# A two-layer encoder with routed experts on one core: whole expert weights in one load, separate bias rows, last rows' loads from ACT, and a first group by columns

## The chip, the cores and the metric

One Trainium2 chip, one of its cores. The time is the device time of one execution in microseconds (us). Lower is better.

## The reference

Two layers over 256 tokens of width 1024, all in float32. Each layer normalises the rows, multiplies them by w_in (1024 x 2304), lets three groups of heads attend (A: a neighbourhood on a grid 64 wide with a learned bias; B: dilated windows; C: grouped queries with rotary positions), and adds the mixed heads times w_out. Then a router picks one of four groups of experts per token and two of the eight experts in it. Every expert is a gated pair of products:

```python
def expert_block(args):
    e, idx = args
    xb = xt[idx]
    return (jax.nn.silu(xb @ w_gate[e]) * (xb @ w_up[e])) @ w_down[e]
...
for l in range(DEPTH):
    x = x + mixer_sublayer(x, norm1_g[l], w_in[l], ..., na_rpb[l], mix_norm_g[l], w_out[l])
    x = x + hier_moe(rms_norm(x, norm2_g[l]), ..., w_gate[l], w_up[l], w_down[l])
```

w_gate and w_up are 1024 x 512 per expert, w_down is 512 x 1024; each is 2 MB, there are 32 experts in a layer, and all of them are loaded. That is 403 MB of expert weights in two layers; everything else is some 33 MB.

## The kernel before, in words

**Memory.** SBUF holds a ring of 16 pieces of 1 MB (8 KB in each of 128 partitions) and, beside it, six regions of the same size that are free once the attention part is over: three in `work`, then `tables`, `biased` and `hT`. `rows` (line 324) gives the memory of a piece; pieces 16 to 21 are those six.

**Items.** The experts of a layer are worked through in 11 items. `KINDS` and `TIME` (lines 75 and 79) give the number of experts in the order of work: 2, 2, 4, 1, 4, 1, 4, 2, 4, 4, 4. Each item has up to 128 places for tokens, shared by its experts. An item has six rounds, the upper and the lower half of w_gate, w_up and w_down, and needs one piece per round and expert. TensorE (PE) gathers the tokens by a matmul with a one-hot matrix (line 951), runs the six rounds (line 989), and brings the result back to x (line 1015). ACT takes the Silu of the gate rounds and copies, VectorE (DVE) makes the one-hot matrices (lines 1715 to 1719), multiplies, and adds to x (line 1750). The six rounds of four experts are 32 matmul instructions each.

**The plan.** `ring_plan` (line 102) is run when the program is built. It deals out the pieces in the order of loading: each load gets the piece that is free first, with the semaphore and value that say so (`p_round` counts rounds, `p_down` the last round's halves, five and two per item). Items up to the eighth may use pieces 0 to 20, later ones 0 to 15. SP issues every load from this plan, in order (`item`, line 529; `piece_in`, line 447, lines 449 to 453 being the waits and the load); a load that has to wait for its piece holds back all that follow. PE waits for the landings of all experts' pieces at the start of a round (line 983). A few pieces around the second and third item are loaded in halves (`half_in`, line 455).

**The last item.** Here PE also runs matmuls with the identity between the rounds (`warm`, line 671). The lower half of w_down comes in three parts (`lower_half_in`, line 467, issued at line 476): the two chunks of rows with the first 512 columns, then one chunk with the other 512, then the other chunk. PE takes the first part at once (`lower_rows`, line 997, matmuls at line 1007), brings back the first half of the result, and then takes the other two.

**The attention part.** w_in is loaded in three groups of 768 columns, C, A and B, 3 MB each, into three adjoining pieces. A group comes as two loads of half the rows (line 515), but the very first one, of layer 1, as four: by columns (the key and value columns 512 to 768, then the query columns 0 to 512) and by halves of the rows (lines 502 to 511). A projection runs in units; the first two use the key and value columns, the next two the query columns (`project`, line 694). The learned bias of group A is built from windows of the rows of na_rpb, each partition reading 250 numbers per head, one number further on than the partition before (`bias_loads`, line 417), which PE spreads by a matmul with a flip matrix (line 727). For layer 1 that is 64 x 4 rows of 250 numbers; for layer 2 it is 64 rows of 1645 numbers, from the first head's window through the last one's, loaded during the last but one item of layer 1 (`staged_loads`, line 408). The router's decisions come from PE, DVE and ACT; before the ranks of the tokens (line 943) PE runs three `warm` calls.

**Order of work.** The engines' programs are written out by hand, the same for both layers, with the semaphores named in the code: `mixers`, `first`, ten items, a loop for experts with too many tokens (not entered with these inputs), and the eleventh item. SP's order of loads in a layer is: w_in's groups with the small tables between them, w_out, then the expert weights.

Of the kernel before, what the change touches and what calls it, by code (L numbers as in the profile page):

```python
# [29 lines left out]
P = 128  # L30
# [8 lines left out]
GRID = 64  # L39
# [52 lines left out]
BESIDE_FREE = [("p_pv", 8, 24)] * 4 + [("p_logit", 2, 40), ("p_pv", 8, 24)]  # L92
TABLES, BIASES, TURNED_ROWS, EARLY = PIECES + 2, PIECES + 3, PIECES + 4, PIECES + 5
# [5 lines left out]
HALVED = {(l, *key): 2 * l + n for l in range(LAYERS) for key, n in (((1, 5, 0), 1), ((1, 5, 1), 2), ((2, 0, 0), 2))}  # L99


def ring_plan():
# [6 lines left out]
    def take(key, n, done, time, allowed):  # L109
        starts = [i for i in allowed if i + n <= max(allowed) + 1 or n == 1]  # L110
# [12 lines left out]
    for l in range(LAYERS):  # L123
# [29 lines left out]
def encoder(nc, a, out):  # L153
    ctx = ExitStack()
    with ctx:
# [12 lines left out]
        tables = sb("tables", [P, PIECE])  # L168
        biased = sb("biased", [P, PIECE])
# [75 lines left out]
        head_step = [250, 465]  # L245
# [3 lines left out]
        beside = [work[:, 0:PIECE], work[:, PIECE:2 * PIECE], tables[:], biased[:], hT_flat, work[:, 2 * PIECE:3 * PIECE]]  # L249
# [106 lines left out]

        block = ctx.enter_context(nc.Block())
# [32 lines left out]
        def _(sp):  # L390
# [26 lines left out]
            def bias_loads(l):  # L417

                first = a["na_rpb"][l:l + 1, 0:1, 4:11, 0:GRID // 2 - 1]
                lo = 15 - (GRID - 1)  # L420
                shape = [[GRID, 4, 250], [GRID, 1, 3 * 465 + 250]][l]
                sp.dma_start(windows[l].rearrange("p (h c) -> p h c", h=shape[1]),
                             bass.AP(first.tensor, first.offset + lo, [[1, GRID], [465, shape[1]], [1, shape[2]]])).then_inc(d_rel, 16)
# [54 lines left out]
            def mixers(l):  # L478
# [4 lines left out]
                for g in range(3):  # L483
# [18 lines left out]
                    if l == g == 0:  # L502

                        for n, (c0, c1) in enumerate(PARTS["C"]):
                            src = a["w_in"][l:l + 1, :, lo + c0:lo + c1].rearrange("l (k p) c -> (l p) k c", k=KD)
                            for half in range(2):
                                ks = slice(half * 4, half * 4 + 4)
                                sp.dma_start(group_in(l, g)[:, ks, c0:c1], src[:, ks]).then_inc(d_lower[n] if half else landed[pos + n], 16)
                                if n == half == 0:
                                    sp.dma_start(x[:, 1], xr[:, 1]).then_inc(d_x[1], 16)  # L510
# [11 lines left out]
                if l:  # L522
                    dil_load(l)
                    route_loads(l)

# [3 lines left out]
            def item(l, i, q):  # L529
# [9 lines left out]
                for r in range(6):  # L539
                    for e in range(n):  # L540
# [7 lines left out]
                        if (l, i, r, e) in HALVED:  # L548
# [4 lines left out]
                            if (i, e) != (1, 1):  # L553
                                half_in(l, i, r, e, ids[e], 1)
                        elif r < 5 or i < NI - 1:
# [1286 lines left out]
```

## Time and profile before

| | us |
|---|---|
| median of 3 runs | 1176.21 |
| lowest and highest | 1175.89, 1178.5 |
| the profiled execution | 1178.81 |
| its span, first to last instruction | 1177.0 |
| TensorE (PE) busy | 997.6 |
| VectorE (DVE) busy | 327.1 |
| ScalarE (ACT) busy | 170.9 |
| GpSimd (POOL) busy | 51.6 |
| bytes moved | 436.80 MB, 371 GB/s on the mean |

The chain of work that ended last has 57% of the span on PE, 31% on loads and 7% on SP's queue. In the rows further down, L12 is line 12 of the kernel, "PEclk" the granted clock of TensorE as a share of full speed, "DMA share" the mean busy share of the 16 DMA engines, and `SPq` the instructions of SP's sequencer, the issues of loads above all; an issue that lasts long is one that was held back. "x32" counts instructions, and a float32 matmul is two of them. The time in square brackets is the engine's idle time before the row and what ended it.

### The profile page before, as it was taken

The numbers are of one execution on the slowest core, as the hardware profiler recorded it, in microseconds if no ns is written. First come the engines' busy times: TensorE is split into PE (matmuls) and PEld (weight loads), VectorE is DVE, ScalarE is ACT, GpSimd is POOL, SyncE is SP. The second block draws the span as 40 slices with busy tenths as digits, with TensorE's granted clock in tenths as the row PEclk, the third lists the DMA queues.
The fourth block names the chain that finished last, engine by engine and source line by source line (L and its number), as shares of the span: only waits on it lengthen the run. The fifth ranks groups of instructions, "written<-read, shape, count | busy, mean of one in ns | idle before, by whom it ended". The sixth has DMA issues, their size and how long they took to land.

```text
span 1177.0 us, 14082 instructions
## 1 busy us (share of the span) xinstructions
PE 997.6 (85%) x5406; PEld 467.7 (40%) x5406; DVE 327.1 (28%) x742; ACT 170.9 (15%) x440; POOL 51.6 (4%) x104
## 2 busy tenths in 40 slices
PE   8999999998977946659899999999969779474686
PEld 5556644353423412114356656444424234131242
DVE  3546543221211200102145555432212112010111
ACT  1344311110000100000014333111100001000000
POOL 2121100000000000000021211000000000000000
PEclk9999999999998987878999999999999989788899
DMA  9863889999999999999998247999999999999997
GB/s 307 331 250 114 351 305 416 421 421 420 422 422 420 420 422 356 420 422 421 406 399 305 104 178 286 357 417 420 421 421 422 420 421 421 422 420 422 421 421 281
DMA packets 78132, 436.80 MB, mean 371 GB/s; under 512 B 12800, under 2 KB 15792, under 8 KB 30704
## 3 DMA queue, kind: packets, MB, share of 16 engines
q1 hardware_dynamic: 78064, 435.87, 91.6%
q8 instruction: 45, 0.74, 0.2%
q14 instruction: 23, 0.19, 0.0%
HBM read 434.79 MB, written 1.05 MB: 370 GB/s over the span
## 4 chain that ended last, share of the span: by engine, by line
PE 57%; DMA 31%; SPq 7%; DVE 2%; issue 1%; POOL 1%; DVEq 0%; ACT 0%; POOLq 0%
PE bank L989 27%; DMA ring<-in_w_up 12%; DMA ring<-in_w_down 11%; PE bank L713 9%; PE bank L951 5%; SPq L453 5%; PE bank L840 5%; PE bank L1015 4%; DMA ring<-in_w_gate 2%; DMA biased<-in_w_down 2%; DMA tables<-in_w_down 2%; DMA ring<-in_w_in 1%; SPq L476 1%; PE bank L786 1%; PE bank L776 1%
## 5 line engine op out<-in xcount | busy, mean ns | idle before, releaser
L989 PE MATMUL bank<-ring,work 128*32 128x512 f32 (+2 forms) x2592 | 483.4, 671 | 153.3 <-DMA ring<-in_w_up 59.8
L989 PEld LDWEIGHTS bank<-ring,work 128*32 128x32 f32 (+2 forms) x2592 | 145.3, 131 | 427.9 <-issue 425.9
L713 PE MATMUL bank<-ring,hT 128*128 128x512 f32 (+1 forms) x384 | 128.3, 488 | 2.4 <-DMA ring<-in_w_in 1.2
L951 PE MATMUL bank<-work,h 128*128 128x128 f32 x704 | 89.9, 284 | 6.6 <-DVE work L1716 5.1
L951 PEld LDWEIGHTS bank<-work,h 128*128 128x128 f32 x704 | 85.2, 198 | 21.9 <-issue 15.2
L713 PEld LDWEIGHTS bank<-ring,hT 128*128 128x128 f32 x384 | 71.3, 190 | 49.9 <-issue 42.2
L1746 DVE COPY work<-bank 128x512 f32<-128x512 f32 x22 | 15.2, 691 | 253.6 <-PE bank L989 251.2
L1015 PE MATMUL bank<-work 128*128 128x512 f32 x176 | 81.4, 604 | 2.4 <-ACT work L1294 1.6
L1736 DVE TENSOR_TENSOR work<-work,bank 128x512 f32<-128x512 f32 x22 | 15.1, 687 | 238.4 <-PE bank L989 238.4
L1750 DVE TENSOR_TENSOR x<-x,bank 128x512 f32<-128x512 f32 x88 | 60.5, 687 | 44.3 <-PE bank L1015 44.3
L840 PE MATMUL bank<-ring,h 128*128 128x512 f32 x128 | 58.2, 600 | 0.0
L989 PE MATMUL bank<-work 128*32 128x512 f32 (+2 forms) x176 | 57.5, 594 | 0.0
L1289 ACT COPY work<-bank 128x512 f32<-128x512 f32 x22 | 12.9, 585 | 273.9 <-PE bank L1057 273.9
L1015 PEld LDWEIGHTS bank<-work 128*128 128x128 f32 x176 | 31.8, 190 | 50.9 <-issue 49.2
L1283 ACT COPY work<-bank 128x256 f32<-128x256 f32 x22 | 8.2, 372 | 299.3 <-PE bank L1039 299.3
L1715 DVE TENSOR_TENSOR work<-iota,work 128x512 f32<-128x512 f32 x20 | 13.8, 692 | 126.4 <-PE bank L1039 125.1
L989 PE MATMUL bank<-biased,work 128*32 128x512 f32 (+1 forms) x80 | 40.6, 655 | 0.0
L1294 ACT COPY work<-bank 128x512 f32<-128x512 f32 x22 | 12.9, 585 | 177.2 <-PE bank L989 159.9
L674 PE MATMUL bank<-ident 128*128 128x384 f32 x94 | 36.2, 531 | 2.8 <-DMA ident<-in_c_ident 2.8
L989 PE MATMUL bank<-hT,work 128*32 128x512 f32 (+1 forms) x80 | 36.3, 597 | 0.0
L989 PE MATMUL bank<-tables,work 128*32 128x512 f32 (+2 forms) x80 | 36.1, 594 | 0.0
L1272 ACT ACTIVATE work<-bank,gain 128x128 f32<-128x128 f32 x88 | 25.1, 368 | 57.9 <-PE bank L951 57.9
(206 smaller groups left out, 708.8 us busy)
## 6 DMA issues: line engine op xcount, KB each, us to landing
ring<-in_w_gate SPq DMA_DIRECT2D x110, 1024.0 KB, 26.0
ring<-in_w_up SPq DMA_DIRECT2D x108, 1024.0 KB, 26.7
ring<-in_w_down SPq DMA_DIRECT2D x100, 1024.0 KB, 26.5
ring<-in_w_in SPq DMA_DIRECT2D x10, 1536.0 KB, 14.8
work<-in_w_up SPq DMA_DIRECT2D x10, 1024.0 KB, 10.3
ring<-in_w_out SPq DMA_DIRECT2D x8, 1024.0 KB, 16.9
work<-in_w_gate SPq DMA_DIRECT2D x8, 1024.0 KB, 17.2
ring<-in_w_down SPq DMA_DIRECT2D x16, 512.0 KB, 12.1
```

What stands on the lines that cost most here:

```text
L453: sp.dma_start(rows(pos, k), w[:, 0, half * k:half * k + k]).then_inc(landed[pos], 16)
L674: matmul(bank[b][:, 0:3 * P].rearrange("p (n s) -> p n s", n=3), ident[:], ident[:].unsqueeze(1).broadcast_to([P, 3, P]), start=True, stop ...
L713: last = matmul(bank[6 + i % 2][:, 0:c1 - c0], hT[:, k, t * P:t * P + P], group_in(l, gi)[:, k, c0:c1], start=(k == 0), stop=(k == KD - 1))
L840: last = matmul(bank[6 + n % 2][:, :], mixed[:, pos0 + c, t * P:t * P + P], rows(pos, 2)[:, c % 2, half * 512:half * 512 + 512], start=(c ...
L951: last = nc.tensor.matmul(bank[k // 4][:, k % 4 * P:k % 4 * P + P], h_kc[:, t, k, :], pick[:, t, :], start=(t == 0), stop=(t == TT - 1))
L989: last = nc.tensor.matmul(bank[b][e * w:e * w + w, :], lhs[:, k, e * w:e * w + w], rows(pos, k_count // 2)[:, kk, n * 512:n * 512 + 512], ...
L1015: last = nc.tensor.matmul(bank[2 + n][:, :], pickT[:, t, :], y[:, half * 512:half * 512 + 512], start=True, stop=True)
L1272: last = nc.scalar.mul(xg[:, k, :], bank[1][:, (k - 4) * P:(k - 3) * P], gain2[:, q // NI, k:k + 1])
L1715: seated(tt(hot, over(iota[:, 0:P], 1, 2 * TT), wide(seats[:, TIME[i], :], P), ALU.is_equal))
L1736: tt(hid, hid, bank[3][:, :], ALU.mult).then_inc(v_hid, 1)
L1746: nc.vector.tensor_copy(y[:, 512:1024], bank[7][:, :]).then_inc(v_y, 1)
L1750: tt(xs, xs, bank[2 + n][:, :], ALU.add).then_inc(v_back[n], 1)
```

## The change

- From the fourth item on, the two halves of a weight are loaded by one instruction of 2 MB (`whole_in`), into two adjoining pieces, and both are free again only after the second half's round. In the last item that holds for w_gate alone. Where all of an item's six loads were one piece each, pieces 0 to 15 can be paired, and 16 with 17 and 18 with 19; piece 20 takes no whole weight. `tables` and `biased` become one tensor `kept`, so that they adjoin. PE waits for a whole weight at its first round and for nothing at its second.
- SP copies layer 2's bias windows, 64 x 4 rows of 250 numbers, to a region `apart` in device memory during layer 1, after w_out's loads; the load for layer 2 reads 64 rows of 1000 numbers from there, after a wait for the copy.
- The third part of the last item's lower w_down half is issued by ACT and no longer by SP, after the Silu and the third round, with ACT's own reads of the experts' numbers.
- The first group of w_in is loaded by columns in layer 2 too.
- PE runs four `warm` calls, not three, before the ranks, and two short matmuls with the identity after them.

```diff
+WHOLE_FROM = 3
+def whole(i, r):
+    return i >= WHOLE_FROM and (i < NI - 1 or r < 2)
...
     def take(key, n, done, time, allowed):
-        starts = [i for i in allowed if i + n <= max(allowed) + 1 or n == 1]
+        starts = [i for i in allowed if i + n <= PIECES or n == 1 or n == 2 and i in (PIECES, TABLES)]
...
-            used[i] += i < pos + 2
+            used[i] += i < pos + (2 if n == 3 else 1)
...
-                    take((l, i, r, e), 1, done, t0 + 100 + 10 * i + r, allowed)
+                    if not whole(i, r):
+                        take((l, i, r, e), 1, done, t0 + 100 + 10 * i + r, allowed)
+                    elif r % 2 == 0:
+                        done = ("p_down", 2 * q + 2) if r == 4 else ("p_round", 5 * q + r + 2)
+                        take((l, i, r, e), 2, done, t0 + 100 + 10 * i + r + 1, allowed)
+                        plan[l, i, r + 1, e] = plan[l, i, r, e][0] + 1, [], []
...
-        tables = sb("tables", [P, PIECE])
-        biased = sb("biased", [P, PIECE])
+        kept = sb("kept", [P, 2 * PIECE])
+        tables, biased = kept[:, 0:PIECE], kept[:, PIECE:2 * PIECE]
...
+        apart = nc.dram_tensor("apart", (GRID, 4 * 250), F32, kind="Internal").ap()
+            def window_rows(l):
+                first = a["na_rpb"][l:l + 1, 0:1, 4:11, 0:GRID // 2 - 1]
+                return bass.AP(first.tensor, first.offset + 15 - (GRID - 1), [[1, GRID], [465, 4], [1, 250]])
+            def windows_apart(l):
+                sp.dma_start(apart.rearrange("p (h c) -> p h c", h=4), window_rows(l)).then_inc(d_apart, 16)
             def bias_loads(l):
...
+                if l:
+                    sp.wait_ge(d_apart, 16)
+                    sp.dma_start(windows[l], apart).then_inc(d_rel, 16)
+                else:
+                    sp.dma_start(windows[l].rearrange("p (h c) -> p h c", h=4), window_rows(l)).then_inc(d_rel, 16)
...
+            def whole_in(l, i, r, e, expert):
+                pos, _, waits = PLAN[l, i, r, e]
+                for name, value in waits:
+                    sp.wait_ge(frees[name], value)
+                w, k = weight(("w_gate", "w_up", "w_down")[r // 2], l, expert)
+                two = (ring[:, pos * PIECE:(pos + 2) * PIECE] if pos < PIECES else work[:, 0:2 * PIECE] if pos == PIECES
+                       else kept[:])
+                sp.dma_start(two.rearrange("p (k c) -> p k c", k=2 * k), w[:, 0]).then_inc(landed[pos], 16)
...
-                ks, cols, done = [(slice(0, 2), slice(0, 512), landed[pos]), (slice(0, 1), slice(512, 1024), d_last[0]),
-                                  (slice(1, 2), slice(512, 1024), d_last[1])][part]
+                ks, cols, done = [(slice(0, 2), slice(0, 512), landed[pos]), (slice(0, 1), slice(512, 1024), d_last[0])][part]
...
-                    if l == g == 0:
+                    if g == 0:
...
                 if l:
                     dil_load(l)
                     route_loads(l)
+                else:
+                    windows_apart(1)
...
-                warm(7, 3)
+                warm(7, 4)
...
+                for _ in range(2):
+                    matmul(bank[7][:, 0:P], ident[:], ident[:], start=True, stop=True)
...
+            def last_rows_in(l):
+                i, n = NI - 1, KINDS[TIME[NI - 1]]
+                act.wait_ge(v_order, 2 * l + 2)
+                act.sem_inc(seen[4], 1)
+                for e in range(n):
+                    r = RANK0[TIME[i]] + e
+                    expert = act.value_load(order[0:1, r:r + 1], min_val=0, max_val=NE - 1)
+                    pos, _, waits = PLAN[l, i, 5, e]
+                    for name, value in waits:
+                        act.wait_ge(frees[name], value)
+                    w = a["w_down"][l:l + 1, bass.ds(expert, 1)].rearrange("l e (p k) c -> p (l e) k c", k=KE)
+                    act.dma_start(rows(pos, 2)[:, 1:2, 512:1024], w[:, 0, 3:4, 512:1024]).then_inc(d_last[1], 16)
...
                 nc.scalar.activation(hid, bank[2][:, :], ACT.Silu).then_inc(a_silu, 1)
+                if i == NI - 1:
+                    act.wait_ge(p_round, 5 * q + 3)
+                    last_rows_in(l)
```

## Rows read from the trace of the kernel before

**Rows 1.** The page: busy time, the DMA row of 40 slices, packets, queues

```profile
PE 997.6 (85%) x5406; PEld 467.7 (40%) x5406; DVE 327.1 (28%) x742; ACT 170.9 (15%) x440; POOL 51.6 (4%) x104
...
DMA  9863889999999999999998247999999999999997
...
DMA packets 78132, 436.80 MB, mean 371 GB/s; under 512 B 12800, under 2 KB 15792, under 8 KB 30704
...
q8 instruction: 45, 0.74, 0.2%
```

**Rows 2.** Busy time, granted clock and DMA rate by stretches (first line: the columns)

```profile
core 0: us, PE busy (x) PEld busy (x) DVE busy (x) ACT busy (x) POOL busy (x), PEclk, DMA share, GB/s
77.00:94.00 17.00, 16.69 (x85) 11.10 (x84) 11.51 (x25) 6.31 (x21) 4.03 (x7) 1.00 0.01 2
14.00:19.00 5.00, 5.00 (x21) 3.65 (x20) 1.38 (x3) 0.73 (x2) 0.13 (x1) 1.00 1.15 224
...
340.00:360.00 20.00, 13.57 (x105) 5.64 (x98) 3.48 (x6) 0.96 (x3) 0.00 (x0) 0.83 1.01 421
459.00:468.00 9.00, 1.59 (x8) 0.46 (x12) 0.00 (x0) 0.00 (x0) 0.00 (x0) 0.64 1.03 211
579.00:585.00 6.00, 4.29 (x40) 1.02 (x32) 0.00 (x0) 0.00 (x0) 0.00 (x0) 1.00 1.06 388
598.00:609.00 11.00, 11.00 (x39) 7.06 (x38) 3.53 (x10) 0.73 (x2) 3.67 (x9) 1.00 1.03 401
...
1163.00:1168.00 5.00, 2.72 (x18) 0.99 (x19) 0.00 (x0) 0.58 (x1) 0.00 (x0) 1.00 0.54 206
140.00:144.00 4.00, 3.94 (x14) 1.96 (x13) 3.48 (x23) 2.08 (x2) 0.00 (x0) 0.59 1.02 420
728.00:732.00 4.00, 4.00 (x24) 4.00 (x24) 2.58 (x15) 0.00 (x0) 0.00 (x0) 0.60 0.16 66
```

**Rows 3.** The chain that ended last, layer 1's fifth item (start us, us, what)

```profile
264.66 5.77 PE bank L989 x53
270.43 26.62 DMA ring<-in_w_down
```

**Rows 4.** PE's instructions in order of time, merged, layer 1 and the hand-over

```profile
207.03 7.07 PE L989 MATMUL bank<-ring,work 128*32 128x512 f32 x64
...
528.13 6.14 PE L989 MATMUL bank<-ring,work 128*32 128x512 f32 x32 [6.30 <-DMA ring<-in_w_down]
...
583.21 1.92 PE L1007 MATMUL bank<-ring,work 128*32 128x512 f32 x16 [1.71 <-DMA ring<-in_w_down]
...
597.57 2.61 PE L713 MATMUL bank<-ring,hT 128*128 128x256 f32 x11 [1.22 <-DMA ring<-in_w_in]
```

**Rows 5.** DMA issues of the bias rows (count, size, us to landing)

```profile
hT<-in_na_rpb SPq DMA_DIRECT2D x1, 411.2 KB, 23.1
...
work<-in_na_rpb SPq DMA_DIRECT2D x1, 250.0 KB, 11.1
```

**Rows 6.** SP's instructions in order of time, layer 1's last rows

```profile
556.39 22.90 SPq L476 DMA_DIRECT2D ring<-in_w_down  x12
```

**Rows 7.** ACT's instructions in order of time: the hidden rows' copy, both last items

```profile
577.22 0.58 ACT L1289 COPY work<-bank 128x512 f32<-128x512 f32 x1 [14.59 <-PE bank L1057]
...
1156.02 0.58 ACT L1289 COPY work<-bank 128x512 f32<-128x512 f32 x1 [16.26 <-PE bank L1057]
```

**Rows 8.** PE's instructions in order of time, the end of layer 2

```profile
1164.49 1.92 PE L1007 MATMUL bank<-ring,work 128*32 128x512 f32 x16 [1.73 <-DMA ring<-in_w_down]
1167.20 1.96 PE L1015 MATMUL bank<-work 128*128 128x512 f32 x4 [0.79 <-ACT work L1294]
```

**Rows 9.** PE's instructions in order of time, around the routers of both layers

```profile
140.14 3.67 PE L674 MATMUL bank<-ident 128*128 128x384 f32 x6
...
144.70 3.81 PE L951 MATMUL bank<-work,h 128*128 128x128 f32 x32 [0.75 <-DVE work L1699]
...
727.72 5.44 PE L951 MATMUL bank<-work,h 128*128 128x128 f32 x32 [0.83 <-issue]
```

More of the change, by code:

```diff
@@ L243, in encoder @@
         flip = [s[0:GRID, 0:P] for s in staged]
-        head_step = [250, 465]
+        head_step = [250, 250]
         windows = [s[0:GRID, P:P + 3 * n + 250] for s, n in zip(staged, head_step)]
         gain_rows = [s[0:3 * KD, P + 3 * n + 250:2 * P + 3 * n + 250] for s, n in zip(staged, head_step)]
-        beside = [work[:, 0:PIECE], work[:, PIECE:2 * PIECE], tables[:], biased[:], hT_flat, work[:, 2 * PIECE:3 * PIECE]]
+        beside = [work[:, 0:PIECE], work[:, PIECE:2 * PIECE], tables, biased, hT_flat, work[:, 2 * PIECE:3 * PIECE]]
         o = [2 * PIECE]
@@ L355, in run_layers @@
                 item(l, NI - 1, l * NI + NI - 1)
+        apart = nc.dram_tensor("apart", (GRID, 4 * 250), F32, kind="Internal").ap()
+        d_apart = sem("d_apart")
         block = ctx.enter_context(nc.Block())
@@ L415, in gain_loads @@
                     sp.dma_start(gain_rows[l][n * KD:(n + 1) * KD], a[name][l:l + 1].rearrange("l (k p) -> (l k) p", p=P)).then_inc(d_gains, 16)
-            def bias_loads(l):
[L419 to L423, printed above, removed]
+            def window_rows(l):
[3 more added lines that the diff above has]
+                sp.dma_start(apart.rearrange("p (h c) -> p h c", h=4), window_rows(l)).then_inc(d_apart, 16)
+            def bias_loads(l):
+                if l:
[3 more added lines that the diff above has]
+                    sp.dma_start(windows[l].rearrange("p (h c) -> p h c", h=4), window_rows(l)).then_inc(d_rel, 16)
                 sp.dma_start(flip[l], a["c_flip"]).then_inc(d_rel, 16)
@@ L508, in mixers @@
                                 sp.dma_start(group_in(l, g)[:, ks, c0:c1], src[:, ks]).then_inc(d_lower[n] if half else landed[pos + n], 16)
-                                if n == half == 0:
+                                if l == n == half == 0:
                                     sp.dma_start(x[:, 1], xr[:, 1]).then_inc(d_x[1], 16)
@@ L554, in item @@
                                 half_in(l, i, r, e, ids[e], 1)
+                        elif whole(i, r):
+                            if r % 2 == 0:
+                                whole_in(l, i, r, e, ids[e])
                         elif r < 5 or i < NI - 1:
@@ L557, in item @@
                 if i == NI - 1:
-                    for part in range(3):
+                    for part in range(2):
                         for e in range(n):
@@ L707, in project @@
                         pe.wait_ge(v_xT, x_turned(l, t, k // 4))
-                    if l == gi == 0:
-                        if i % 2 == 0 and k % 4 == 0:
-                            pe.wait_ge(d_lower[i // 2] if k else landed[pos + i // 2], 16)
+                    if gi == 0:
+                        if i % 2 == 0 and k == 0:
+                            pe.wait_ge(landed[pos + i // 2], 16 * count[i // 2])
+                        elif i % 2 == 0 and k == 4:
+                            pe.wait_ge(d_lower[i // 2], 16 * (l + 1))
                     elif i % 4 == 0 and k % 4 == 0:
@@ L982, in round_of @@
                         pos, count, _ = PLAN[l, i, r, e]
-                        pe.wait_ge(landed[pos], 16 * count[0])
+                        if count:
+                            pe.wait_ge(landed[pos], 16 * count[0])
                     for n, b in enumerate(banks):
```

## The prediction

> **What bounds the kernel now.** I read the slices first: TensorE is busy 85% of the span, and the DMA row is at nine tenths or more except in the attention part of each layer, slices 2 to 6 and 22 to 25 of 40 [rows 1]. By stretches of 20 us the stream of expert weights runs at 421 to 422 GB/s with a DMA share of 1.01 [rows 2]. So most of the time is bytes over a rate: a megabyte piece (1.049 MB) takes 1.049 / 0.421 = 2.49 us. The chain of waits says the same in another way: TensorE consumes 5.77 us of matmuls, and then a w_down load that its round set free is on the chain for 26.62 us [rows 3]; at 2.49 us a piece that load stood behind some ten others, so the chain's length there is the queue's depth and not an idle stream. In the attention part the stream stops for want of free pieces and TensorE's order of work is the bound; whatever starts that part later moves the end one for one.
>
> **Whole weights.** The trace has 78132 packets, of which 30704 are under 8 KB [rows 1]. The other 47428 are nearly all the 8 KB runs of the pieces, one per partition (128 x 370 = 47360). A whole weight is one run of 16 KB per partition, in memory and in the two neighbouring pieces, so its packets can be twice as long; the q8 queue has 45 packets in 0.74 MB, so packets of 16 KB do exist here [rows 1]. The price of a packet comes from three run lengths. On one of 16 engines an 8 KB packet takes 8192 / (421/16) = 311 ns; a 3 KB one (w_in, 401 GB/s) 123 ns; a 2 KB one (column halves, 388 GB/s) 84.5 ns [rows 2]. From 2 to 8 KB that is 0.0369 ns a byte and 9 ns a packet whatever its length, and the 3 KB row fits (0.0369 x 3072 + 9 = 122). A layer has 20 experts x 3 + 4 = 64 whole weights; each saves 128 packets, 8 per engine. Two layers: 128 x 8 x 9 ns = **9.2 us**. The bounds are 0 (packets are cut at 8 KB as now, or the rate is held elsewhere) and 10; I take 9.2, since the three lengths lie on one line and nothing in the trace is flat at the top.
> The Trainium skill, DMA: Bandwidth & Descriptors, section Bandwidth, states that loads from HBM are bound at about 358 GB/s per core by the memory, and not by the fabric. By that rule a longer packet buys nothing; the measured 421 lies above that figure, so the measurement decides.
>
> Does the coarser freeing starve the stream? The tightest place is the fourth and fifth item. The 24 pieces of the fifth item end at 297.05 [rows 3], so they begin at 297.05 - 24 x 2.49 = 237.3, and its second whole w_down is due 18 pieces later, at 282. Its buffer is free when the same item's gate is done: 264.66 + 7.07 (64 instructions, two rounds) = 271.7 [rows 3, 4]. Ten us are left. In the last three items there are 16 pieces: eight are in flight (19.9 us) while TensorE uses the other eight in 7.07 us, or about 10 with the clock at its lower level on waking, as in the 6.14 us for a round that takes 3.54 [rows 3, 4]. Again some 10 us are left, so I cost it at nothing.
>
> **Bias rows apart.** The second layer's rows are now read as one overlapping window of 411 KB, 64 runs each starting 4 bytes after the last [rows 5]. In the 9 us around its landing the stream moved 211 instead of 421 GB/s at a full DMA share [rows 2]: 9 x (1 - 211/421) = 4.5 us lost. The 250 KB of the first layer show the same at 14 to 19 us: 224 GB/s, a loss of 2.3 us [rows 2]. Afterwards 250 KB of separate 4000-byte rows are loaded: 0.4 us less in bytes. If the copy reads as slowly as the first layer's rows, 4.5 + 0.4 - 2.3 = 2.6 us are gained; if at the full rate, 4.9. If the slow stretch belongs to the gains and the flip matrix loaded beside it, 0. I take **4.2**. The copy itself lies behind w_out's loads, ahead of first-item pieces that wait for no semaphore; its 3 to 5 us delay those, and the 17 idle us from 77 to 94 (2 GB/s) [rows 2] absorb it. Without that cover it would cost up to 5. SP's wait for it comes 380 us later and holds nothing.
>
> **Last rows begun by ACT.** SP issues twelve loads for the last w_down rows from 556.39 on and is held 22.90 us by the full queue [rows 6]. ACT now issues four of them, 1 MB, after the third round, with four register reads. ACT then has nothing to do until it copies the turned hidden rows, before which it sat idle for 14.59 and 16.26 us in the two layers [rows 7]; most of that lies behind the third round, so the issues are hidden up to some 10 us. Its loads go into another queue and need not stand behind SP's backlog; they then arrive early, and what was ahead moves back by 1.049 / 0.388 = 2.7 us. What moves back matters: TensorE waits 1.73 us for the first column half at 1164.49, then has 12.5 us to the end of the span, and the very last rows are hardly waited for: the matmuls on them follow the step back at 1167.20 without a wait of their own [rows 8]. So the second layer's tail gets **2.7 us longer** (bounds 0, if the queue order stays as issued, and 2.7). The Trainium skill, DMA: Bandwidth & Descriptors, section Queues, rings and completion order, says that each DMA engine takes turns between the queues it has work for; by that the term is the upper bound. No row here shows two busy queues.
>
> **The hand-over to layer 2.** Today TensorE has done the first w_down round of the tenth item when the second one's pieces land, and spends 6.14 us on the latter [rows 4]. Afterwards both rounds follow the last landing: 3.5 us more. Adding, seating, the gather and the last item's rounds, filled with warming matmuls, run on from there almost without a pause to the wait of 1.71 us at 583.21 [rows 4], so 3.5 - 1.7 = 1.8 us remain. The overtaking moves that same wait by 2.7; the larger counts, 2.7. Against that stands the load by columns: the first unit waits 1.22 us for the second half of w_in's rows [rows 4]; its 256 columns (1 MB of 3) now come first, 5 us sooner, and that wait goes. What is late next is x itself, turned by the same instructions. The query columns, all landed at 597.5 today and 0.6 later in shorter runs, are needed only after 16 matmuls per row block, past 601. Sum: 2.7 - 1.2 = **+1.5 us** (bounds -1.2 and +2.7). In the second layer the 3.5 us vanish in idle time before the last item's later rounds.
>
> **Warming matmuls.** One more call ahead of the ranks, and two short ones after them. Three calls take 3.67 us in the first layer [rows 9], where the granted clock is 0.59 on the mean [rows 2], near its lower level of 1.2 GHz; the ranks follow at once, so a fourth is worth up to +1.2 us. In the second layer TensorE idles after them, the clock falls to 0.60 on the mean [rows 2], and the gather takes 5.44 instead of 3.81 us [rows 9]: up to -1.6 if it now stays at 2.4 GHz. The two short ones lie in waits of 0.75 and 0.83 us for the picks [rows 9]. I take 0 (bounds -1.6 and +1.2).
>
> **Sum.** -9.2 - 4.2 + 2.7 + 1.5 + 0 = -9.2 us against the profiled execution's 1178.8 us (1.8 around a span of 1177.0): 1169.6. That execution is 2.6 us above the median of the runs, 1176.2, so the forecast is **1167.0**. About 0.2%, 2.4 us, is what a measurement can tell from no change.
>
> **Rivals.** (a) *ACT's loads do not push the others back, or the pushed ones were not the bound.* Then the tail costs 0 and the hand-over 1.8 - 1.2 = 0.6: -9.2 - 4.2 + 0.6 = -12.8, 1163.4. For it: the stream still drains unevenly at 206 GB/s from 1163 to 1168 [rows 2], and part of the landing is that; against: the separate queue. Chance 0.28. (b) *No longer packets, or no faster ones:* -4.2 + 4.2 = 0, 1176.2. For it: q1 shows none over 8 KB. Chance 0.14. The Trainium skill's figure on memory, named above, would end here. (c) *The stream runs dry for want of whole buffers.* In the last three items a weight's eight pieces are free only after both rounds; if TensorE's turn-round passes 19.9 us less about 2 for a load to begin, each of the seven weights of four experts after the first two pays the excess. It decides from a turn-round of 18 us; 1.5 us too much at 7 x 2 weights is 21 us, and with the rest 1176 - 9 + 21 = 1188. Against it: 7 to 10 us as worked out. Chance 0.10. The forecast itself gets 0.45, and 0.03 goes to the tail being some us longer than summed.
>
> **How the numbers follow.** Faster: 0.45 + 0.28 + 0.03, and about 0.03 of (b), where the bias rows give more: 0.79. Slower: (c) and a little of (b), 0.12. Same: 0.09. Range: at the low end (a) with its bounds, -9.2 - 4.9 - 1.2 - 1.6 = -16.9, 1159.3; at the high end (b), 1176.5. That leaves out (c) and the edges.
>
> **What would show it.** Right: about 63,000 packets in place of 78,000 (16,384 fewer, some more for the columns); stretches of whole weights at 427 GB/s (16384 / (605 + 9) ns x 16); no 211 GB/s stretch before 470; a DMA share of 1 from 200 to 600; the first w_down wait 2 to 3 us later against the stream, and no wait for w_in in the second layer. Wrong: packets unchanged at 421 GB/s; a DMA share below 0.95 in the last three items with SP waiting for TensorE; a gather of 5.4 us still in the second layer; ACT's issues taking over 10 us.

## The result, and the profile after

The kernel after takes 1169.47 us (median of 5 runs, 1167.71 to 1171.24), the one before 1176.85 in runs of the same sitting. The ratio is 0.9935, with a 95% interval from 0.992 to 0.9951: 7.6 us faster, where 9.2 were forecast. The profiled execution of after is the lowest of its five, 1167.71 with a span of 1165.9 us.

The page of after: busy time, granted clock and DMA row in 40 slices, packets and queues.

```profile
PE 990.7 (85%) x5418; PEld 466.4 (40%) x5418; DVE 327.1 (28%) x742; ACT 171.1 (15%) x440; POOL 51.7 (4%) x104
...
DMA  9953889999999999999997247999999999999996
...
DMA packets 61026, 436.86 MB, mean 375 GB/s; under 512 B 10800, under 2 KB 15072, under 8 KB 29984
...
q1 hardware_dynamic: 59808, 433.86, 90.7%
q10 hardware_dynamic: 1152, 2.10, 0.5%
```

There are 17,106 packets fewer for nearly the same bytes [rows 1], and a second busy queue: q10 holds ACT's eight loads, 2.10 MB. Next, stretches of after (span of the stretch, busy times, granted clock, DMA share, GB/s).

```profile
340.00:360.00 20.00, 15.25 (x128) 5.49 (x121) 2.92 (x5) 0.87 (x2) 0.00 (x0) 0.91 1.01 430
445.00:475.00 30.00, 19.52 (x128) 8.61 (x120) 4.81 (x7) 2.32 (x6) 0.00 (x0) 0.83 1.01 395
579.00:585.00 6.00, 5.21 (x35) 1.63 (x28) 1.62 (x3) 0.59 (x1) 0.00 (x0) 1.00 1.08 375
1150.00:1155.00 5.00, 1.68 (x20) 0.50 (x16) 0.00 (x0) 0.00 (x0) 0.00 (x0) 1.00 0.60 224
```

The first row answers to the 421 GB/s of [rows 2]; over stretches of 40 us from 240 to 440 us it is 427 to 428. The third covers the same times as the 388 of [rows 2] but not the same loads: in after it takes in the columns of w_in, with runs of 1 KB. The column halves of w_down, from 568 to 576 us, move at 386 GB/s. Around the bias rows the stream is still slow. PE's instructions of after in order of time: both gathers, the hand-over, and the end of layer 2.

```profile
143.51 3.81 PE L992 MATMUL bank<-work,h 128*128 128x128 f32 x32 [0.33 <-DVE work L1758]
...
572.61 3.64 PE L1031 MATMUL bank<-ring,work 128*32 128x512 f32 x32 [0.68 <-ACT work L1348]
578.17 1.92 PE L1049 MATMUL bank<-ring,work 128*32 128x512 f32 x16 [1.92 <-DMA ring<-in_w_down]
...
588.87 1.99 PE L752 MATMUL bank<-ring,hT 128*128 128x256 f32 x8 [0.80 <-DVE hT L1398]
...
591.14 12.21 PE L752 MATMUL bank<-ring,hT 128*128 128x256 f32 x40
...
721.24 3.81 PE L992 MATMUL bank<-work,h 128*128 128x128 f32 x32 [0.29 <-issue]
...
1146.43 3.64 PE L1031 MATMUL bank<-ring,work 128*32 128x512 f32 x32 [2.43 <-DMA ring<-in_w_down]
1153.40 1.92 PE L1049 MATMUL bank<-ring,work 128*32 128x512 f32 x16 [3.32 <-DMA ring<-in_w_down]
```

Two rows of before that answer to these, the last item's fifth round and the first projection of layer 2:

```profile
577.86 3.64 PE L989 MATMUL bank<-ring,work 128*32 128x512 f32 x32 [0.68 <-ACT work L1289]
...
593.91 1.99 PE L713 MATMUL bank<-ring,hT 128*128 128x256 f32 x8 [0.80 <-DVE hT L1339]
```

From the first gather to the first projection of layer 2 it is 445.36 us (before 449.21), on to the second gather 132.37 (133.81), and from there to the end of the span 444.66 (449.28) [rows 4, 8, 9]. With 1.2 us up to the first gather that makes the 11.1 us by which the two spans differ. The wait for w_in of [rows 4] is gone, the wait in the tail is longer, 3.32 instead of 1.73 us [rows 8], and both gathers take 3.81 us [rows 9]. Last, ACT's and SP's issues of the last rows in layer 1:

```profile
560.92 3.60 ACTq L1323 DMA_DIRECT2D ring<-in_w_down  x4
571.98 0.59 ACT L1348 COPY work<-bank 128x512 f32<-128x512 f32 x1 [14.59 <-PE bank L1099]
```

```profile
553.00 18.32 SPq L508 DMA_DIRECT2D ring<-in_w_down  x8
```

ACT's four issues take 3.60 us inside an idle time that is not longer than before [rows 7]; they hold up nothing on ACT. But they land early. The last item's loads of layer 1 in after (issues from 550 to 575 us: KB each, median us from issue to landing):

```profile
ring<-in_w_down SPq DMA_DIRECT2D x4, 512.0 KB, 21.5
ring<-in_w_down ACTq DMA_DIRECT2D x4, 256.0 KB, 8.6
```

The first column half, issued from 553.00 us on, takes 21.5 us; ACT's loads, issued from 560.92 on and needed last, take 8.6.

### The profile page after: what moved, and what is told of

Its sections match the earlier page's. It is cut to its first block, busy times and chain, and to the rows that moved or that the text cites. A ratio compares the mean times of both kernels' runs of the same rounds, so it can differ in the third digit from the quotient of the medians.

```text
span 1165.9 us, 13783 instructions
## 1 busy us (share of the span) xinstructions
PE 990.7 (85%) x5418; PEld 466.4 (40%) x5418; DVE 327.1 (28%) x742; ACT 171.1 (15%) x440; POOL 51.7 (4%) x104
## 2 busy tenths in 40 slices
DMA packets 61026, 436.86 MB, mean 375 GB/s; under 512 B 10800, under 2 KB 15072, under 8 KB 29984
## 4 chain that ended last, share of the span: by engine, by line
PE 61%; DMA 33%; DVE 3%; SPq 1%; issue 1%; POOL 1%; ACT 0%; DVEq 0%; POOLq 0%
PE bank L1031 30%; DMA ring<-in_w_down 13%; DMA ring<-in_w_up 10%; PE bank L752 9%; DMA ring<-in_w_gate 8%; PE bank L879 5%; PE bank L1057 4%; PE bank L992 4%; DMA work<-in_w_down 2%; PE bank L711 2%; PE bank L825 1%; PE bank L815 1%; SPq L498 1%; PE bank L847 1%; PE bank L1049 1%
## 5 line engine op out<-in xcount | busy, mean ns | idle before, releaser
L1031 PE MATMUL bank<-ring,work 128*32 128x512 f32 (+2 forms) x2608 | 476.8, 664 | 139.1 <-DMA ring<-in_w_up 50.1
L1031 PE MATMUL bank<-work 128*32 128x512 f32 (+2 forms) x192 | 83.7, 625 | 6.0 <-DMA ring<-in_w_down 6.0
L1031 PE MATMUL bank<-kept,work 128*32 128x512 f32 (+2 forms) x176 | 81.3, 615 | 5.4 <-DMA ring<-in_w_up 5.4
L1031 PEld LDWEIGHTS bank<-work 128*32 128x32 f32 (+2 forms) x192 | 22.5, 130 | 31.0 <-issue 30.6
L879 PEld LDWEIGHTS bank<-ring,h 128*128 128x128 f32 x128 | 23.2, 190 | 25.3 <-issue 25.0
```

The lines of the kernel that those rows point to most:

```text
L879: last = matmul(bank[6 + n % 2][:, :], mixed[:, pos0 + c, t * P:t * P + P], rows(pos, 2)[:, c % 2, half * 512:half * 512 + 512], start=(c ...
L1031: last = nc.tensor.matmul(bank[b][e * w:e * w + w, :], lhs[:, k, e * w:e * w + w], rows(pos, k_count // 2)[:, kk, n * 512:n * 512 + 512], ...
```

## The experiments

Each kernel is the one after the change with one edit, or with several where it says so. Ratios are to the kernel before, from runs on the same chip; the intervals are 95%. 0.1% is 1.18 us.

**Whole weights undone.**

```diff
-WHOLE_FROM = 3
+WHOLE_FROM = NI
```

> The changed kernel with every expert weight loaded as two pieces again, all else kept. Theory, a fixed price per packet: about 77,000 packets, the stream of expert weights back at 421 GB/s in place of 427 to 428, and the time 7 to 9 us above the changed kernel's 1169.5, at 1176 to 1179; the two rounds of w_down in the tenth item end some 3 us sooner against the stream. Rival, the gain is from elsewhere (bias rows, columns, the warming call): 1169 to 1172 and the rate hardly moves.

1179.87 us, ratio 1.0022 [1.001, 1.0035]. Against after that is 0.87%, 10.2 us: whole weights carry more than the whole gain, and what is left of the change is 2.6 us slower than the kernel before. This takes back their price at the hand-over as well as their gain.

**The same plan and waits, but each whole weight as two loads with 8 KB runs.** This separates the length of a run from the plan and from the coarser freeing, but not from the number of loads.

```diff
-        if key in HALVED:
+        if key in HALVED or n == 2:
...
-                sp.dma_start(two.rearrange("p (k c) -> p k c", k=2 * k), w[:, 0]).then_inc(landed[pos], 16)
+                for half in range(2):
+                    ks = slice(half * k, half * k + k)
+                    sp.dma_start(two.rearrange("p (k c) -> p k c", k=2 * k)[:, ks], w[:, 0, ks]).then_inc(landed[pos], 16)
```

> The changed kernel's plan, buffers and waits, but each whole weight is issued as two loads of 1 MB, with runs of 8 KB. It tells run length from the plan and from the number of loads. Theory, a fixed price per packet: packets as in the kernel before, 421 GB/s, and 1178 to 1181, since the coarser waits stay without their gain. Rival, fewer issues or the other order of buffers make the gain: 427 GB/s and 1169 to 1171 with halves as well if it is the plan; if it is the number of issues, SP is seen to issue with gaps in the DMA share.

1180.45 us, ratio 1.0033 [1.0022, 1.0045]. Its page and its stretch from 340 us on:

```profile
DMA packets 79460, 436.89 MB, mean 371 GB/s; under 512 B 12848, under 2 KB 17120, under 8 KB 32032
```

```profile
340.00:360.00 20.00, 13.49 (x107) 4.01 (x110) 3.07 (x6) 0.87 (x2) 0.00 (x0) 0.83 1.01 421
```

The rate is back at 421 GB/s with the 18,434 packets, and the gain is gone: 0.98%, 11.5 us against after. So the plan doesn't make it. Of the packets, 16,384 are the halved 8 KB runs and 2,048 are under 512 B (12,848 here, 10,800 in after), 16 for each of the 128 loads that whole weights save. The DMA share is 1.01 with and without them, so the stream doesn't wait for issues; how the gain divides between longer runs and fewer small packets no run shows. The coarser waits cost 1.3 us by the ratios (0.11%), in intervals that overlap, so nothing is a possible value and 3 us is too.

**All last rows issued by SP again.**

```diff
-                ks, cols, done = [(slice(0, 2), slice(0, 512), landed[pos]), (slice(0, 1), slice(512, 1024), d_last[0])][part]
+                ks, cols, done = [(slice(0, 2), slice(0, 512), landed[pos]), (slice(0, 1), slice(512, 1024), d_last[0]),
+                                  (slice(1, 2), slice(512, 1024), d_last[1])][part]
...
-                    for part in range(2):
+                    for part in range(3):
...
-                if i == NI - 1:
-                    act.wait_ge(p_round, 5 * q + 3)
-                    last_rows_in(l)
```

> The changed kernel with the third part of the last w_down rows issued by SP again, behind the other parts. Theory, overtaking: ACT's megabyte pushed the first column half back by 2.7 us in each layer; without it the wait at the first of the last matmuls begins 2.5 to 3 us sooner against the stream in layer 2 and about 1 us sooner in layer 1, and the time is 1164 to 1167. Rival, the landing of the first column half is set by the drain of the slowest DMA engines, whatever the order: 1168.5 to 1170.5.

1166.24 us, ratio 0.9911 [0.9897, 0.9925]. Run again later, as the base of three others:

> The same kernel as the one with the last rows issued by SP, run again as the base of the other three, and to tell whether it beats the change as a whole on a second chip run: the first gave 0.9911 of before, with its interval below the change's 0.9935. Theory (ACT's loads overtake SP's and cost 2 to 3 us in the tail): 0.990 to 0.992 again. Rival (the first difference was the spread of the runs): near 0.9935.

1164.11 us, ratio 0.9891 [0.9872, 0.991]. Both intervals lie below the ratio of after, 0.9935, though the first overlaps after's own interval a little: without ACT's loads the kernel is 2.8 to 5.2 us faster, and it beats both kernels of this case. PE in its first run, hand-over and tail:

```profile
574.60 3.64 PE L1032 MATMUL bank<-ring,work 128*32 128x512 f32 x32 [0.68 <-ACT work L1346]
578.05 1.90 PE L1050 MATMUL bank<-ring,work 128*32 128x512 f32 x16
...
1144.43 3.64 PE L1032 MATMUL bank<-ring,work 128*32 128x512 f32 x32 [0.68 <-ACT work L1346]
1149.86 1.93 PE L1050 MATMUL bank<-ring,work 128*32 128x512 f32 x16 [1.79 <-DMA ring<-in_w_down]
```

In the tail of this execution the fifth round waits for no load, and the first column half comes at 1149.86 instead of 1153.40, 3.5 us. Counted from the second gather, it comes after 432.2 to 432.6 us in the four kernels with whole weights and ACT's loads, and after 428.3 to 429.4 in the five with whole weights, SP's loads and the same gather: 3.4 us. The bytes are the same; only the order in which they land differs. The last item's loads of layer 1 with all of them by SP:

```profile
ring<-in_w_down SPq DMA_DIRECT2D x4, 512.0 KB, 18.9
ring<-in_w_down SPq DMA_DIRECT2D x8, 256.0 KB, 7.6
```

The first column half takes 18.9 us here and 21.5 with ACT's loads; in layer 2 it is 17.9 and 21.0. So in both layers ACT's loads overtake it, by 2.6 and 3.1 us.

At the hand-over PE waits for no w_down load at all. From the start of the fifth round to the first column half it is 3.45 or 3.46 us in the six kernels with whole weights and SP's loads, and 5.56, 5.62, 4.19 and 5.82 in the four with ACT's: the push costs 0.7 to 2.4 us there too. That the spans of after and of this run differ by no more than the tail's 3.5 us is the choice of execution: after's had reached the fifth round 2 us sooner, at 572.61.

**No whole weights, and no loads by ACT.** The two edits above together.

> No whole weights and all last rows issued by SP: what is left of the change is the bias rows, the column order and the warming calls. The kernel with no whole weights but with ACT's loads took 1.0022 of before. Theory: ACT's loads cost the same 2.8 us here as beside whole weights, ratio 1.0022 - 0.0024 = 0.9998, so the bias rows' 3.2 us would be eaten by something else, the columns or the warming. Rival: without whole weights ACT's loads cost more, up to 5.5 us, as the hand-over and the tail both wait for the stream there; ratio 0.997 to 0.998, and the bias rows keep their gain.

1173.55 us, ratio 0.9962 [0.9947, 0.9977]. The rival came true, and by more than it said: without whole weights ACT's loads cost 0.60%, 7 us. The last two waits for w_down with ACT's loads, and without them:

```profile
1159.73 6.12 PE L1031 MATMUL bank<-ring,work 128*32 128x512 f32 x32 [3.85 <-DMA ring<-in_w_down]
1165.67 1.90 PE L1049 MATMUL bank<-ring,work 128*32 128x512 f32 x16
```

```profile
1153.73 3.64 PE L1032 MATMUL bank<-ring,work 128*32 128x512 f32 x32 [1.47 <-DMA ring<-in_w_down]
...
1159.15 1.92 PE L1050 MATMUL bank<-ring,work 128*32 128x512 f32 x16 [1.78 <-DMA ring<-in_w_down]
```

The column halves are on time there; it is the round ahead of them that the overtaking makes late, and after its 3.85 us of idling it runs 6.12 instead of 3.64 us. In layer 1 the same round starts at 578.00 instead of 575.92 and runs 5.16 instead of 3.64 us. So both layers pay, and more than with whole weights, as the slower clock comes on top in both. This settles what puzzled at first, why the other parts looked worse than nothing.

**Whole weights alone:** ACT's loads, the bias rows, the column order and the warming calls all as before.

> Whole weights alone: the bias rows of the second layer as an overlapping window of 411 KB, all last rows issued by SP, the first group by rows, three warming calls. If the parts add up as the runs so far price them (whole weights 10 us, and the hand-over 1.2 longer by them), this is near 1177 - 10 + 1 = 1168, ratio 0.992. As I predicted the parts: 9.2 for the packets and 1.8 for the hand-over, ratio 0.9937. Rival: whole weights pay more in this kernel than beside the other parts, since what the other parts add is not hidden there: ratio 0.989 to 0.990.

1168.1 us, ratio 0.9911 [0.9891, 0.9931]: 10.5 us, between the sum of the parts and the rival. The spans of the profiled executions add up: before 1177.0, whole weights alone 1167.7 (-9.3), everything but whole weights and ACT's loads 1171.7 (-5.3), both 1162.4 (-14.6). The ratios give 12 us for both together (0.9911 and 0.9891) where the parts make 15; each has an interval of about 2 us either way. Beside the other parts and SP's loads, whole weights are thus worth 6.0 to 8.4 us by the ratios (0.9962 against 0.9911 and 0.9891), less than alone. The end of layer 1 in whole weights alone:

```profile
578.29 3.64 PE L1026 MATMUL bank<-ring,work 128*32 128x512 f32 x32 [0.68 <-ACT work L1340]
581.75 1.90 PE L1044 MATMUL bank<-ring,work 128*32 128x512 f32 x16
```

Before, the fifth round started at 577.86 and the first column half at 583.21: at this place the faster stream has brought nothing up to the fifth round, and 1.5 us once the wait of 1.71 is gone.

**The bias rows as one window of 411 KB again,** beside ACT's loads and without them.

```diff
-        head_step = [250, 250]
+        head_step = [250, 465]
...
-                    sp.wait_ge(d_apart, 16)
-                    sp.dma_start(windows[l], apart).then_inc(d_rel, 16)
+                    first = a["na_rpb"][l:l + 1, 0:1, 4:11, 0:GRID // 2 - 1]
+                    sp.dma_start(windows[l], bass.AP(first.tensor, first.offset + 15 - (GRID - 1), [[1, GRID], [1, 3 * 465 + 250]])).then_inc(d_rel, 16)
...
-                else:
-                    windows_apart(1)
```

> The changed kernel with layer 2's bias rows read as the overlapping window of 411 KB again and no copy. In the changed kernel's trace the stream loses about 2.2 us around the separate rows, where the kernel before lost 4.5, so the theory as it now stands: 4.5 us lost again plus 0.4 for the bytes, +2.3 to +2.8 us, 1172. Rival, as forecast, +4.2: 1173.7. Rival, the slow stretch belongs to the gains and the flip matrix: +0.4.

> Last rows issued by SP, and the second layer's bias rows as one overlapping window of 411 KB again. Beside ACT's loads the window's profile lost 2 us up to the w_down wait at the hand-over and another 2.9 us behind it, where a 128-column matmul group took 3.7 instead of 1.96 us, which is the clock and not the rows. Theory: the bias rows alone are worth 1.7 us (1.3 in the rate of 450 to 466 us, 0.4 in bytes), so this is 0.9925 if the base is 0.9911. Rival: they are worth the 4.2 us I predicted: 0.9947.

Beside ACT's loads 1172.76 us, ratio 0.9962 [0.9949, 0.9976], 3.2 us behind after; without them 1166.57, 0.9906 [0.9889, 0.9924], 2.5 us behind its base by the medians and 1.8 by the ratios, whose intervals overlap. From the first gather to the first projection of layer 2 it is 446.26 us there, and 443.30 to 444.57 in the three kernels with rows apart and SP's loads. So the rows are worth about 2 us.

**Only 25 of the 1000 bias columns loaded.** The second layer's biases are left out for the most part.

```diff
-                    sp.dma_start(windows[l], apart).then_inc(d_rel, 16)
+                    sp.dma_start(windows[l][:, 0:25], apart[:, 0:25]).then_inc(d_rel, 16)
```

> Last rows issued by SP; of the second layer's bias rows only the first 25 of 1000 columns are loaded from the copy, 100 bytes a partition instead of 4000, so its neighbourhood biases are left out for the most part. With all of them the stream still falls to about 220 GB/s for 3 us at 457 to 460. Theory: the slow stretch belongs to the rows (250 KB in 64 partitions), so it goes, and the time falls by 0.6 us of bytes and about 2 us of rate: 0.9911 becomes 0.989. Rival: it belongs to the gains and the flip matrix loaded beside them (24 runs of 512 bytes, 64 of 512 bytes): then the stretch stays and the time falls by 0.6 us, 0.9906.

1162.13 us, ratio 0.9868 [0.985, 0.9885], 2.0 us faster than its base by the medians, in intervals that overlap; up to the first projection of layer 2 it is 442.01 us. The stretch from 445 to 475 us, which takes in all of the staged loads, in four kernels, one fence each: before; all last rows by SP; the same with the 411 KB window; the same with few rows.

```profile
445.00:475.00 30.00, 20.33 (x130) 8.69 (x123) 3.11 (x5) 2.31 (x6) 0.00 (x0) 0.78 1.02 356
```

```profile
445.00:475.00 30.00, 19.38 (x136) 8.62 (x128) 4.83 (x7) 2.32 (x6) 0.00 (x0) 0.89 1.01 390
```

```profile
445.00:475.00 30.00, 20.55 (x140) 8.91 (x132) 4.15 (x7) 2.31 (x6) 0.00 (x0) 0.83 1.01 375
```

```profile
445.00:475.00 30.00, 18.73 (x128) 8.40 (x120) 4.82 (x7) 2.31 (x6) 0.00 (x0) 0.89 1.01 421
```

Against 427 GB/s the last three lose 30 x (1 - 390/427) = 2.6 us with 250 KB, 3.7 with 411 KB and 0.4 with 25 columns; before loses 4.6 against its 421. The slow stretch belongs to the rows and not to the gains or the flip matrix. Per KB it is 10.4 ns with rows apart (9.0 in after), 9.0 in the overlapping window (11.2 before), and 9.2 in layer 1 (2.3 us for 250 KB [rows 2]): within that spread **the rows are as slow apart as they were overlapping, and the gain is that there are fewer bytes of them.** If so, loading the 64 x 4 windows of 250 straight from na_rpb, as in layer 1, would give the same without a copy. That was not tried.

The Trainium skill, SBUF — State Buffer, section Door 1: The DMA port swizzle, says that a transfer to partitions 0 to 63 reaches half of the ports and so moves at half the rate. The trace agrees in direction; but by that rule the 256,000 bytes would lose an estimated 0.6 us, and 2.2 are lost. What makes the rest stays open.

**The first group of layer 2 by rows again,** beside ACT's loads and without them.

```diff
-                    if g == 0:
+                    if l == g == 0:
...
-                    if gi == 0:
+                    if l == gi == 0:
...
```

> The second layer's first group is loaded by rows again, in two halves of 1.5 MB as before the change, and its first unit waits for both; all else is as after the change (1169.5 us, 0.9935 of before). Theory as predicted: the column order removed a wait of 1.22 us, so this comes out 1.2 us longer, about 1170.7 and a ratio near 0.9945. Rival, raised by the sum of the runs so far, which leaves about 3 us unexplained: the columns cost more than they save, because their rows of 1 and 2 KB move slower than rows of 3 KB (3.15 MB at 388 instead of 401 GB/s is 0.3 us) and the load ahead of the later units is cut finer; then this is 0.5 to 3 us shorter, ratio 0.991 to 0.993.

> Last rows issued by SP, and the second layer's first group by rows again. Beside ACT's loads the row order measured 0.9937 against 0.9935, too near to tell. Theory as predicted: the column order is worth 1.2 us, the wait for w_in; so this is 0.9921 if the base is 0.9911. Rival: the first group is complete in time in either order, since the stream reaches it a few us sooner with whole weights; no difference, 0.9911.

1170.52 us, ratio 0.9937 [0.9919, 0.9955]; and 1164.89, 0.9893 [0.9876, 0.9909]. The second is 0.8 us behind its base by the medians and 0.02% by the ratio: no difference that can be told. In neither does PE wait for w_in in layer 2; the second one's first projection:

```profile
587.72 1.99 PE L751 MATMUL bank<-ring,hT 128*128 128x256 f32 x8 [0.81 <-DVE hT L1394]
...
589.99 12.21 PE L751 MATMUL bank<-ring,hT 128*128 128x256 f32 x40
```

**Three warming calls, and none behind the ranks.**

```diff
-                warm(7, 4)
+                warm(7, 3)
...
-                for _ in range(2):
-                    matmul(bank[7][:, 0:P], ident[:], ident[:], start=True, stop=True)
```

> Three warming calls ahead of the ranks and none behind them, as before the change; all else as after it. Theory as predicted: nothing, 1169.5 and 0.9935, within bounds of 1.6 us longer (the second layer's gather takes 5.44 us again instead of 3.81) and 1.2 us shorter. Rival: the warm clock in the second layer is what the calls give, and with three calls the gather there goes back to 5.4 us: 1171 and 0.995.

1172.98 us, ratio 0.9949 [0.9932, 0.9966], 0.14% or 1.6 us behind after, in intervals that overlap. The traces say it more surely. Over all profiled executions the gather takes 3.81 us in each of the 22 with four calls (11 kernels, two layers), and 5.44 in 4 of the 6 with three. The gathers of whole weights alone:

```profile
143.53 5.44 PE L987 MATMUL bank<-work,h 128*128 128x128 f32 x32 [0.88 <-DVE work L1750]
...
724.80 5.44 PE L987 MATMUL bank<-work,h 128*128 128x128 f32 x32 [0.83 <-issue]
```

**A clock fall behind the wait for the first column half.** With three calls and ACT's loads, the profile shows this at the hand-over to layer 2 (PE in order of time, then the stretch's clock):

```profile
580.99 2.64 PE L1047 MATMUL bank<-ring,work 128*32 128x512 f32 x16 [2.18 <-DMA ring<-in_w_down]
584.40 3.75 PE L1055 MATMUL bank<-work 128*128 128x512 f32 x4 [0.77 <-ACT work L1351]
```

```profile
582.00:588.00 6.00, 5.23 (x16) 1.18 (x5) 0.69 (x1) 0.59 (x1) 0.00 (x0) 0.50 1.07 374
```

After 2.18 us of idling the clock is granted at 0.50, its lower level of 1.2 GHz, and two groups that take 1.92 and 1.96 us in after take 2.64 and 3.75. The 411 KB window beside ACT's loads shows the same (3.12 and 3.71 behind a wait of 1.98); after itself idles 1.92 us there and keeps 2.4 GHz. ACT's loads are not needed for it. The tail of the kernel with few bias rows, where SP issues everything:

```profile
1147.27 2.76 PE L1050 MATMUL bank<-ring,work 128*32 128x512 f32 x16 [2.22 <-DMA ring<-in_w_down]
1150.81 3.75 PE L1058 MATMUL bank<-work 128*128 128x512 f32 x4 [0.77 <-ACT work L1351]
```

In all, PE waits 1.9 us or more for a first column half in nine places of the profiled executions. In four the next matmuls ran at full clock (waits of 1.92, 2.04, 2.69 and 3.32 us), in five they did not (1.98, 2.18, 2.22, 2.74 and 2.83 us), which cost 1.4 to 3 us. At the other places, where PE waited 1.79 us or not at all, they ran at full clock. With whole weights and SP's loads only one place in twelve had so long a wait, with whole weights and ACT's loads seven in eight: so the wait that ACT's loads make costs nothing or up to 3 us more, from one execution to the next.

## Why the prediction was right, and where its terms were off

**Right on the whole,** and on the mechanism of the largest term. *Whole weights, -9.2:* 10.2 measured beside ACT's loads and 10.5 alone, but 6.0 to 8.4 beside the other parts with SP's loads. These runs hold the hand-over's 1.8 us too, so what was forecast for them is 7.4. The rate rose to 427 to 428 GB/s over long stretches, where 427 was worked out, and with 8 KB runs in the same plan it was 421 again. The price of 9 ns a packet held beyond the three lengths it was taken from. The count was short: whole weights alone save 18,433 packets and not 16,384, as each load saved takes 16 small ones with it. If those had the same price, the term would have been 10.4 us; that is an estimate. Rival (b) falls with this. The Trainium skill's bound of 358 GB/s by the memory (DMA: Bandwidth & Descriptors, Bandwidth) is not what holds here: the same stream went from 421 to 427 with longer runs and fewer packets. The same section gives that figure for two cores that stream from one memory at once, and here one core runs.

*No starving:* the DMA share stays at 1 up to the hand-over, and the coarser waits with the old run length cost 1.3 us by the ratios, which can't be told from nothing; rival (c) needed 21. It falls.

*Last rows by ACT, +2.7:* the mechanism was right, the term too small. They overtake SP's backlog; the tail is 3.4 us longer, counted from the second gather, and the whole kernel 2.8 to 5.2 us by the ratios, hand-over included. I priced the 1 MB that goes ahead at 388 GB/s, 2.7 us; the landings moved by 2.6 and 3.1 us. What makes the rest of the 3.4 stays open. One thing was missing: the wait that grows can drop the clock, which the next matmuls pay. Rival (a), at 1163.4, was this term at zero; the kernel with SP's loads lands there or some 2 us above, by its two ratios; the change doesn't. The Trainium skill, DMA: Bandwidth & Descriptors, section Issuing engines are not separate DMA queues, says that issuing from several engines only saves the issuing time. For bandwidth the traces agree, 375 and 370 GB/s from 579 to 585 us with and without ACT's loads; for the order of landing it doesn't hold, and the order cost 3.4 us in the tail. The section on queues, by which the engines take turns, is the one that fits.

*Bias rows, -4.2:* what failed is the choice within the bounds. I took a value near the upper end, as if the copy's separate rows would load at nearly the full rate; they load as slowly per byte as the overlapping ones, and 1.8 to 2.5 us without ACT's loads is what the runs give, at or a little below the lower value of 2.6 (3.2 beside them, with a clock fall in the profiled execution). I had the row that said so in [rows 2]: layer 1's rows are separate and were just as slow.

*Hand-over, +1.5:* near in size, with its parts off. The column order removed nothing beside whole weights, as the wait for w_in is gone with rows too, in all three kernels that have rows; the credit of 1.2 was no gain of the columns. Of the two delays, the round that now follows the last landing is part of what the runs on whole weights measured: in whole weights alone the fifth round starts 0.4 us later than before although the stream is faster (its first gather ends 0.5 us later). ACT's push comes on top, 0.7 to 2.4 us instead of 2.7.

*Warming, 0:* -1.6 in the ratio, in intervals that overlap. The upper and the lower bound were both in the rows; I weighed them as equal, but the fourth call of 0.7 us lies beside work of the other engines (in layer 2 PE's wait for DVE ahead of the ranks is 0.41 us with it and 1.05 without), while the gather's 1.6 us lie on the path.

*The sum:* with the terms as measured beside each other, and 1.5 for ACT's push at the hand-over, -10.2 - 2.2 + 3.4 + 1.5 + 0 - 1.6 = -9.1. The ratio shows -7.6, with an interval from -9.4 to -5.8; the two profiled executions show -11.1, as before's is 2 us above its median and after's 1.8 below. After's profiled execution kept its clock at both column halves. The three other kernels with whole weights of 16 KB runs and ACT's loads lost it at one or both, for 1.4 to 4.4 us; that the usual execution of after does so too would fit, and is argued and not shown. That the forecast came so near was luck in part, because its errors had both signs: bias rows 2 us too good, ACT's loads in the tail 0.7, the columns and the push at the hand-over 1.8 together, warming 1.6 too bad, whole weights with their hand-over up to 3 too bad.

## What to carry to other kernels

Where a stream of loads is the bound, take the fixed price of a packet from stretches with different run lengths, and lengthen the runs before anything else: here 16 KB instead of 8 KB, with half the loads, gave 6 to 12 us of 1177, from one pair of kernels to the next. A load issued by a second engine goes into a second queue and overtakes what the first has in flight; give it only what is needed before that backlog, never what is needed last. And price a load that slows the stream by its bytes, from the row of a load of the same shape.

## What the runs showed of the hardware

- The rate of the full stream follows the length of the runs: 386 to 388 GB/s at 2 KB, 401 to 406 at 3 KB, 421 at 8 KB, 427 to 428 at 16 KB. From 579 to 585 us, where w_in's first group comes in, it is 363 to 377 with columns (1 KB runs) and whole weights, and 394 to 399 with rows (three kernels).
- A load takes 16 packets under 512 B besides its data: 128 loads fewer go with 2,048 such packets fewer.
- Loads that ACT issued overtook SP's that were in flight: 256 KB landed 8.6 us after its issue, while SP's 512 KB, issued before it, took 21.5 instead of 18.9.
- Loads of 4000 or 6580 bytes into each of 64 partitions cost the stream 9 to 11 ns per KB beyond their own share, overlapping or not. I had not expected that of separate rows.
- The length of a PE wait didn't decide whether the clock stayed at 2.4 GHz: after 3.32, 2.69 and 2.04 us it did, after 1.98, 2.18 and 2.22 it did not, and the price was 1.4 to 3 us. With the fourth warming call, the four in 22 cases in which the clock fell did so inside the warming (4.3 to 4.5 instead of 2.8 us), and the gather behind it was spared.
